# Modulation rows in single 128x512 parts beside the first feed-forward's pairs, and norm vectors loaded one chunk earlier

## The reference

```python
# end of the first block; FFN_HIDDEN = D_FF = 2816
gu = einsum('bsd,df->bsf', x, w_gu); gate, up = gu[..., :2816], gu[..., 2816:]
ffn = einsum('bsf,fd->bsd', silu(gate) * up, w_down)
x = layer_norm(ALPHA * x + ffn, ln2_g, ln2_b)
# second block
mod = silu(c) @ w_cond + b_cond            # c: (1, 1024), w_cond: (1024, 6144)
shift_m, scale_m, gate_m, shift_f, scale_f, gate_f = split(mod, 6)
h = rmsnorm(x, g_mix_pre) * (1.0 + scale_m) + shift_m
proj = h @ w_in                            # then attention, pooling, w_out
x = x + gate_m * rmsnorm(mix, g_mix_post)
h = rmsnorm(x, g_ffn_pre) * (1.0 + scale_f) + shift_f
f = (silu(h @ w_gate) * (h @ w_up)) @ w_down
x = x + gate_f * rmsnorm(f, g_ffn_post)
```

## Time and profile before

| | |
|---|---|
| median of three runs | 2593.52 us |
| the profiled execution | 2598.05 us, its span 2596.3 us |
| TensorE, weight loads | 2424.2 us busy (93%), 1957.4 us (75%) |
| VectorE, ScalarE, GpSimd | 1513.9 us (58%), 930.5 us (36%), 687.4 us (26%) |
| mean granted clock of TensorE | 0.968 of full speed |
| chain that ended last | PE 73%, DVE 17%, ACT 3%, DMA 3% |

### The profile page before, as it was taken

How to read it: one execution, slowest core, us unless ns; L and a number is a source line. 1 busy time by engine, 2 the same in 40 slices (tenths; PEclk the granted TensorE clock), 3 DMA queues, 4 the chain that set the end, 5 groups by cost and what they waited for, 6 DMA issues and landing times.

```text
span 2596.3 us, 31339 instructions
## 1 busy us (share of the span) xinstructions
PE 2424.2 (93%) x12119; PEld 1957.4 (75%) x12119; DVE 1513.9 (58%) x2557; ACT 930.5 (36%) x1704; POOL 687.4 (26%) x389
## 2 busy tenths in 40 slices
PE   7999988878999999988998998987989999999998
PEld 6667877777888778766886776665868888888886
DVE  2698888652765767765226316777376555544225
ACT  3556636651222222221112315555333332232112
POOL 2012210000234445421223311012123545442220
PEclk9999988989999999999999999998989999999999
DMA  5014541204314344365222310001232222333224
GB/s 161 17 49 151 190 166 60 95 23 155 124 59 124 119 142 130 114 234 186 100 82 106 106 33 17 25 25 65 71 108 65 74 89 82 95 117 130 98 73 146
DMA packets 215947, 259.99 MB, mean 100 GB/s; under 512 B 15580, under 2 KB 145132, under 8 KB 215800
## 3 DMA queue, kind: packets, MB, share of 16 engines
q1 hardware_dynamic: 215800, 258.00, 30.1%
HBM read 198.14 MB, written 59.82 MB: 99 GB/s over the span
## 4 chain that ended last, share of the span: by engine, by line
PE 73%; DVE 17%; ACT 3%; DMA 3%; issue 2%; POOL 1%; SPq 1%; DVEq 0%; ACTq 0%; POOLq 0%
PE bank L1873 8%; PE bank L558 8%; PE bank L1875 8%; PE bank L1874 8%; PE bank L560 8%; PE bank L559 8%; PE bank L534 5%; PE bank L535 5%; PE bank L536 5%; PE bank L1395 2%; DVE rest L2514 2%; DVE junk L1110 2%; DVE res L1330 1%; PE bank L577 1%; DVE score L1083 1%
## 5 line engine op out<-in xcount | busy, mean ns | idle before, releaser
L515 POOL TENSOR_TENSOR wl<-raw,wh 128x1024 fp32r<-128x1024 f32 x117 | 294.9, 2536 | 1393.9 <-ACT wh L498 1393.9
L558 PE MATMUL bank<-wh,yh 128*128 128x512 f32 x768 | 305.1, 397 | 19.3 <-DVE sum3l L1838 8.6
L559 PE MATMUL bank<-wl,yh 128*128 128x512 f32 x768 | 302.2, 393 | 0.0
L560 PE MATMUL bank<-wh,yl 128*128 128x512 f32 x768 | 302.0, 393 | 0.0
L498 ACT ACTIVATE wh<-raw 128x1024 fp32r<-128x1024 f32 x117 | 122.8, 1056 | 319.2 <-PE bank L560 254.3
L1873 PE MATMUL bank<-yh,wh 128*128 128x512 f32 x576 | 225.7, 392 | 2.3 <-DVE res L2023 2.3
L510 POOL TENSOR_TENSOR wl<-raw,wh 128x512 fp32r<-128x512 f32 x108 | 160.4, 1498 | 253.6 <-ACT wh L495 253.6
L510 POOL TENSOR_TENSOR wl<-res,wh 128x512 fp32r<-128x512 f32 x144 | 194.9, 1375 | 118.6 <-ACT wh L495 98.3
L1875 PE MATMUL bank<-yh,wl 128*128 128x512 f32 x576 | 224.2, 389 | 0.0
L1874 PE MATMUL bank<-yl,wh 128*128 128x512 f32 x576 | 224.1, 389 | 0.0
L558 PEld LDWEIGHTS bank<-wh,yh 128*128 128x128 f32 x768 | 146.0, 190 | 56.6 <-DVE sum3l L1838 9.4
(11 more groups left out here) (341 smaller groups left out, 5425.0 us busy)
## 6 DMA issues: line engine op xcount, KB each, us to landing
raw<-in_w_gu SPq DMA_DIRECT2D x44, 512.0 KB, 4.1
raw<-in_w_down SPq DMA_DIRECT2D x44, 512.0 KB, 3.6
raw<-in_w_in SPq DMA_DIRECT2D x40, 512.0 KB, 4.0
early<-in_w_cond SPq DMA_DIRECT2D x36, 512.0 KB, 3.8
qk_d<-res SPq DMA_DIRECT2D x36, 512.0 KB, 5.0
raw<-in_w_gate SPq DMA_DIRECT2D x22, 512.0 KB, 4.2
raw<-in_w_up SPq DMA_DIRECT2D x22, 512.0 KB, 4.2
res<-in_x SPq DMA_DIRECT2D x16, 512.0 KB, 8.9
```

The lines of the kernel that those rows point to most:

```text
L515: pool.i.tensor_tensor(wl[n % NU][:, :], raw_of(u)[:, :], wh[n % NU][:, :].bitcast(F32), ALU.subtract).then_inc(*po.up(("wl", u)))
L558: pe.i.matmul(bank[:, 0:wide], xa, h[:, c:c + wide], start=k == 0, stop=False)
L559: pe.i.matmul(bank[:, 0:wide], xa, l[:, c:c + wide], start=False, stop=False)
L560: last = pe.i.matmul(bank[:, 0:wide], xb_, h[:, c:c + wide], start=False, stop=k == nk - 1)
```

## The change

There are 96 single pieces ("parts") in place of 48 double ones, all of them in the pairs of layer 1: six to a pair, behind the products `s` = 0, 1, 2, 4, 5 and 6 of the pairs 0 to 15. The two `early` buffers are used in turn; SP loads part h + 2 once VectorE has used part h. The matmul of a row stands behind the product at which its successor's second part is taken, the negation ahead of that row's fifth part, and the rest follows in pairs 16 and 17 (row 11's matmul at (16, 0), its negation at (16, 2), the reload of the whole row with its bias at (16, 4), the addition at (17, 4), the store at (17, 6)). The "R" units are gone from the plan. The vectors are split in two: the loads that need nothing new move to the middle of the third chunk, those that wait for the gain stay ahead of the last.

```diff
-        early_row = sb("early", 1024)
-        early = [early_row[:, 512 * i:512 * i + 512] for i in range(2)]
+        early = [sb(f"early{i}", 512) for i in range(2)]
...
-                    if layer == 1 and not a:
-                        units += mod_rows(m, ROWS[n])
-                        m += ROWS[n]
...
+        N_PART = 96
+        part_at = {slot: h for h, slot in enumerate((q, s) for q in range(16) for s in (0, 1, 2, 4, 5, 6))}
+
+        def pe_mod(q, s):
+            h = part_at.get((q, s), N_PART + 1 if (q, s) == (16, 0) else 0)
+            if h % 8 == 1 and h > 1:
+                n = h // 8 - 1
                 bank = X["r"].open(("mod", n))
                 pe.wait_ge(*X["r"].prior(("mod", n)))
-                pe.wait_ge(*dv.after(("row", 4 * n + 3)))
+                pe.wait_ge(*dv.after(("part", 8 * n + 7)))
...
+        def dve_mod(q, s):
+            if (q, s) == (16, 2):
+                dve_mod_row(11)
+            if (q, s) == (17, 4):
+                dve.wait_ge(*mod_in.after("mod"))
+                dve.i.tensor_tensor(macc[0][:, 0:48], macc[0][:, 0:48], macc[0][:, 64:112], ALU.add).then_inc(*dv.up("mod_whole"))
...
+            h = part_at[q, s]
+            n, k = h // 8, h % 8
+            a, w = macc[n % 2], early[h % 2]
+            if k == 4 and n:
                 dve_mod_row(n - 1)
-            if q == 0 and n >= 2:
+            if k == 0 and n >= 2:
                 dve.wait_ge(*mod_out[n % 2].after(("mod", n - 2)))
...
+        def sp_mod_part(h):
+            sp.wait_ge(*early_out[h % 2].after((1, 3, h % 2)))
+            sp.i.dma_start(early[h % 2][:, :], T["w_cond_2"][h % 8 * 128:h % 8 * 128 + 128, 512 * (h // 8):512 * (h // 8) + 512]
+                           ).then_inc(*row_in[h % 2].up(h, 16))
...
+            h = part_at.get((q, s), N_PART)
+            if h % 8 == 7 and h > 8:
+                sp_mod_row(h // 8 - 1)
+            if h + 2 < N_PART:
+                sp.wait_ge(*dv.after(("part", h)))
+                sp_mod_part(h + 2)
...
                 if a == 18:
-                    before_last()
+                    before_last[1]()
                 if a < 18:
                     for n in range(2):
                         for tb in range(8):
+                            if a == 12 and n and not tb:
+                                before_last[0]()
...
         def sp_vectors2():
-            sp.wait_ge(*mm.after(("down", 1, 12, 1, 7)))
+            sp.wait_ge(*mm.after(("down", 1, 6, 1, 7)))
...
+        def sp_shift2():
             sp.wait_ge(*dv.after("gain2"))
             sp.i.dma_start(sh[:, :], row(0)).then_inc(*ln2_in.up("shift", 16))
...
         def sp_vectors4():
-            sp.wait_ge(*mm.after(("down", 2, 12, 1, 7)))
+            sp.wait_ge(*mm.after(("down", 2, 6, 1, 7)))
```

More of the change, by code:

```diff
@@ L217, in build @@
         hid_in = [sem(f"hid_in{i}") for i in range(8)]
-        row_in = sem("row_in")
+        row_in = [sem(f"row_in{i}") for i in range(2)]
         xb_in = [sem(f"xb_in{i}") for i in range(4)]
@@ L409, in ahead @@
                     before = raw_units[loads - NRAW] if NRAW <= loads < len(raw_units) else None
-                    if loads < NRAW or before is not None and (
-                            before <= m if plan[before][0] == "R" else split_no[last_split(before)] < splits):
+                    if loads < NRAW or before is not None and split_no[last_split(before)] < splits:
                         loads += 1
@@ L440, in sp_feed @@
                     before = raw_units[n - NRAW]
[L441 to L445, removed]
+                    sp.wait_ge(*av.after(("wh", last_split(before))))
+                    sp.wait_ge(*po.after(("wl", last_split(before))))
                 for o, i in load_pairs(raw_units[n]):
@@ L1673, in sp_mod_row @@
                            ).then_inc(*mod_out[n % 2].up(("mod", n), 16))
-        def sp_mod(j):
-            if j % 4 == 3 and j > 4:
-                sp_mod_row(j // 4 - 1)
-            if j >= N_ROW:
-                sp_feed(mod_units[j - N_ROW])
-            else:
-                sp.wait_ge(*dv.after(("row", j - 1)))
-                for half in range(2):
-                    sp.wait_ge(*early_out[half].after((1, 3, half)))
-                r, c = j % 4 * 256, 512 * (j // 4)
-                sp.i.dma_start(early_row[:, :].rearrange("p (k c) -> p k c", k=2),
-                               T["w_cond_2"][r:r + 256, c:c + 512].rearrange("(k p) c -> p k c", p=128)).then_inc(*row_in.up(j, 16))
@@ L1717, in after_down @@
         def after_down(layer, a, kk, n):
-            u = down_units[layer][n][(a + kk) // 2 - 1]
-            return u + (ROWS[n] if layer == 1 and not a else 0)
+            return down_units[layer][n][(a + kk) // 2 - 1]
         turned_in = {1: "y", 2: "x3"}
@@ L1896, in pe_ffn @@
                 pe_pair(layer, q)
-                if layer == 1:
-                    for j in (2 * q, 2 * q + 1):
-                        pe_mod(j)
-            j = N_ROW
             for a, kk in CHUNKS:
@@ L2082, in dve_ffn @@
                         dve.i.tensor_tensor(dst, uses.held[key][:, :], dst, ALU.add).then_inc(*dv.frees(uses, key))
-                    if layer == 1 and not a and tb < ROWS[n]:
-                        dve_mod(j)
-                        j += 1
                     f = next_hidden(a, n, tb)
@@ L2090, in dve_ffn @@
                         after_block(tb)
-                if layer == 1 and a == 0:
-                    dve_mod_row(11)
-                if layer == 1 and a == 6:
-                    dve_mod_last()
         def sp_residual():
@@ L2834, in sp_program @@
             sp_out1()
-            sp_ffn(1, sp_vectors2, sp_norm2)
+            sp_ffn(1, (sp_vectors2, sp_shift2), sp_norm2)
             sp_vu()
```

108 lines of the change are left out of this document (37 added, 71 removed).

## The result

| | before | after |
|---|---|---|
| median beside each other | 2593.9 us (4 runs, 2591.0 to 2596.5) | 2567.6 us (4 runs, 2565.8 to 2573.0) |
| profiled execution, its span | 2598.05, 2596.3 us | 2569.1, 2567.3 us |

The ratio is 0.990 with a 95% interval of 0.9883 to 0.9917. The forecast was 2552, its range 2546 to 2564: the sign is right, the size is not. 26 us came, where 41 were forecast, and the time lies outside the range. The spans of the two profiles differ by 29.0 us.

The account below looks back on a forecast made before the run. TensorE, busy 93% of the span, was taken as the bound, time being lost in its waits or lower clock. +0.5 − 26.1 − 14.0 − 1.7 = −41.3 us off 2593.5 gave 2552 us, range 2546 to 2564.

Parts of the forecast that it names:

- Pairs, +0.5 us: Layer 1's pairs: twelve row matmuls at 1.2 us, 14.2 us in place of 13.7; bounds −1.2 and +6.8.
- VectorE's 85 us of spare time absorb it: Layer 1's pairs: parts landing about 1 us late, some three times in two pairs, stay hidden by VectorE's spare time.
- the first rival: Pairs: the row matmul waits in mid pair, +6.8 in place of +0.5, with late hand-over 2559 us; chance 0.11.
- the second rival: Pairs: SP's waits for GpSimd hold the parts, slower than before, 2630 us; chance 0.04.
- Pairs to down stage and first chunk, −26.1: Layer 1's hand-over (−8.0) and first down chunk (−18.2, less 0.1) become layer 2's; bounds −26.5 and −20.5.
- the fourth rival: First down chunk: the residual holds it, −20.5 in place of −26.1, 2558 us; chance 0.06.
- Norm vectors, layer 1, −14.0: Last chunk into next projections: earlier vector loads end VectorE's 15.87 us wait, 14.0 us gained; bounds 17.5 and 8.3.
- The third rival: Layer 1's norm stage: GpSimd's splits or the turns set TensorE's pace, −8.3 in place of −14.0, 2558 us; chance 0.08.
- Second attention, 0: Second block's attention, between layer 1's projections and layer 2's pairs: no change forecast, 0 us.
- Norm vectors, layer 2, −1.7: Layer 2's last chunk to the end: VectorE's 4.72 us vector wait goes, 1.7 us gained; bounds −1.8 and −1.0.

Follow-up runs that it names:

- e3: The kernel before with only the modulation row's matmul moved, to behind a pair's second product instead of its last; 2587.5 us.
- e15: The changed kernel with a row's store two slots earlier and each modulation part's load issued ahead of the weight refill; 2561.1 us.
- e13: The kernel before, unchanged, profiled once more; 2594.2 us.
- e1: The kernel before with only the norm vectors' edit, the split of the vector loads; 2583.7 us.
- e14: The changed kernel with VectorE's scaling of each block in layer 1's last chunk cut from 1024 to 8 columns; 2565.8 us.
- e6: The changed kernel with the second turn's copy put ahead of the three weight splits in ScalarE's queue, in layer 1's last chunk; 2568.2 us.
- e8: The changed kernel run again without any edit; 2568.1 us.
- e4: The changed kernel without the twelve one-column matmuls, so the sums over the partitions are not made; 2571.0 us.
- e10: The changed kernel without the twelve one-column matmuls and with a row's store two slots earlier; 2564.6 us.
- e12: The changed kernel with four one-moving-column matmuls per row sum, all rows kept on chip, and part loads issued ahead of weight refills; 2558.4 us.

## Why the prediction was wrong

- **Pairs, +0.5 us: the step that failed, +6.1.** The price of a matmul was right (1.18 in e3, 1.19 in e15, 1.2 forecast), and so was the vanished wait. What failed is "VectorE's 85 us of spare time absorb it". Spare time was taken as a sum over the stage, but VectorE cannot work ahead of a part that isn't there, and at the end of a row TensorE asks for the last part two slots behind its place. A part that is later than that stops TensorE at once, whatever time VectorE has to spare elsewhere: 3.8 us in two places, with the low clock behind the longer one. The forecast saw the first rival's mechanism and gave it 0.11, and named SyncE's waits for GpSimd as the second rival; what came is both together, in small. The second rival's sum was wrong in itself: at the mean wait of 6.8 us its 102 us already exceed the 85 of spare time, so by its own terms it decides from a mean of 6.1 us on (2.7 + 85/25) and not from 7.8; such a sum over the stage says neither when nor how much TensorE waits. The forecast also left out the store of the row: 18.9 us of VectorE's waits hung on a step that the working does not mention. e15, with both out of the way, has the 356.7 us that the forecast gave (about 357).
- **Pairs to down stage and first chunk, −26.1: right on its own profile** (−26.7), and the residual did not hold the chunk (the fourth rival did not come). But 83.5 us was the longest of four profiles of that chunk; against e13 the same term is 8.75 + 81.0 − 65.5 = 24.3, against e1 23.0.
- **Norm vectors, layer 1, −14.0: −10.6.** The wait went as forecast. I let VectorE's earlier start of 12.9 us and more come through, with its 7 to 8 us per block written down and not followed to the end: it falls 1.6 us a block behind TensorE, more once the turns' subtractions come, and e14 gives 3.5 us back when VectorE has 1.28 us less a block. The third rival (bound 8.3) was partly right: TensorE's waits in that stretch are for turns (4.4 us in four) and hardly for GpSimd (0.3). But what makes the turns late is in good part VectorE's work, and little of it ScalarE's order (e6: 0.4 to 0.7 us).
- **Second attention, 0: +3.3 in the profiles** (+4.2 in e8). Not forecast, not settled.
- **Norm vectors, layer 2, −1.7: −1.1**, inside its bounds.
- **From the profile to the median.** The forecast took the profiled execution's terms off the median. But that execution was 4.5 us above its median, and part of this lay in a stretch that the change shortens (2.5 us of the first chunk, against e13); the profiled execution after is 1.5 us above its own. That is 3.0 of the 15.6 us missed, 0.2 is the forecast's rounding (2552.2), and the terms above are 12.3 (5.6 pairs, 3.4 norms, 3.3 attention; the rest cancels).
- **The range** held the losses of two rivals together, and the two that came in the pairs and at the norm vectors (5.6 and 3.4 us) would have left the time inside it, at about 2561. It is outside by two things that had no term at all: the attention's 3.3 us and the 3.0 us from the profile to the median.
- **The price of a load.** The prediction names 2.0 us plus bytes over 436 GB/s from the page "DMA: Bandwidth & Descriptors" of the Trainium skill; the page's section on the anatomy of one DMA states this for transfers that GpSimd issues, and these are SyncE's. Its 2.6 us for 256 KB, and the working's own 2.7, lie below the median of 3.1 us here.

## What to carry to other kernels

Spare time of an engine is spent locally: when a stage's load is made of small pieces through two buffers, follow one piece from the release of its buffer through the queue that issues its load, and price what stands ahead of it there; e15 got 7 us by exchanging two calls and moving one store. Where taking out a cost brings nothing (e4), look for the second one that it covered, and add up the stage with what follows it: e10's pairs and e12's were shorter, and their hand-overs longer. And profile the old kernel twice before taking a stretch's excess as a term: here one stretch took 83.5 and 81.0 us in the kernel before, and 79.3 and 79.7 in two others with the same instructions there.

## What was not expected of the hardware

- Four matmuls with one moving column and 128x128 of the row as the stationary side (x8: two passes each) are little cheaper than one with the row's 512 columns moving. Row 1's sum in e12, and below it in e15, neither of them after a wait:

```profile
840.30 0.39 PE L1864 MATMUL bank<-sum4h,wl 128*128 128x512 f32 x1
840.52 0.95 PE L1627 MATMUL bank<-con,macc 128*128 128x1 f32 x8
841.33 0.49 PE L1862 MATMUL bank<-yh,wh 128*128 128x512 f32 x1
```

```profile
840.41 0.39 PE L1860 MATMUL bank<-sum4h,wl 128*128 128x512 f32 x1
840.73 1.02 PE L1625 MATMUL bank<-macc,con 128*1 128x512 f32 x2
841.67 0.50 PE L1858 MATMUL bank<-yh,wh 128*128 128x512 f32 x1
```

From the product's last matmul ahead of it to the next product's first pass 1.03 and 1.26 us, 0.80 and 1.03 more than a step of 0.227; by the pairs' length (354.32 − 342.49)/12 = 0.99 us a row in e12 against 1.19 in e15. The expectation of 0.5 us was wrong.
- With the same instructions (2571 or 2572 matmuls in the profile), the second attention took 480.6 to 486.8 us over eighteen profiles, the first down chunk of before 79.3 to 83.5 over four, and the changed kernel's pairs 361.2 to 365.6 over five.
